# GpSimd adds the squares of two channel tiles in each norm, and the matmul of ones sums the pairs

## What is computed

```python
def rmsnorm(x, gain):
    y = xf * lax.rsqrt(jnp.mean(xf * xf, axis=-1, keepdims=True) + RMS_EPS)
    return (y * gain.astype(jnp.float32)).astype(x.dtype)
...
h = h + 0.5 * swiglu_ffn(rmsnorm(h, ffn1_norm[i]), ffn1_w_in[i], ffn1_w_out[i])
u = rmsnorm(h, mix_norm[i])
y = stick_breaking_attention(u, sb_w_qkv[j], sb_w_o[j], valid)
h = h + y
h = h + 0.5 * swiglu_ffn(rmsnorm(h, ffn2_norm[i]), ffn2_w_in[i], ffn2_w_out[i])
...
h = rmsnorm(h, final_norm)
```

## Time and profile before

| | before |
|---|---|
| median of the runs | 2130.8 us |
| the profiled execution | 2127.97 us, span 2126.2 us |
| PE busy | 1965.9 us, 92% |
| DVE busy | 1097.4 us, 52% |
| POOL busy | 1004.0 us, 47% |
| ACT busy | 686.4 us, 32% |
| mean granted TensorE clock | 0.972 |

### The profile page before, as it was taken

How to read it: one execution, slowest core, us unless ns; L and a number is a source line. 1 busy time by engine, 2 the same in 40 slices (tenths; PEclk the granted TensorE clock), 3 DMA queues, 4 the chain that set the end, 5 groups by cost and what they waited for, 6 DMA issues and landing times.

```text
span 2126.2 us, 35378 instructions
## 1 busy us (share of the span) xinstructions
PE 1965.9 (92%) x12808; PEld 1786.1 (84%) x12808; DVE 1097.4 (52%) x1584; ACT 686.4 (32%) x1226; POOL 1004.0 (47%) x671
## 2 busy tenths in 40 slices
PE   4699999999999985999979999959999999899997
PEld 4699999999999975999978887747777777788886
DVE  5455455554555555334368880174444444454445
ACT  5322222222111124222279882142222222221212
POOL 4554454454534416445467763164454544543340
PEclk8899999999999997999999999979999999999999
DMA  3122222223322200332322212002222222233221
GB/s 120 31 65 84 89 65 84 82 72 125 120 80 83 96 20 21 109 109 95 105 81 67 82 52 60 20 5 84 74 79 84 70 83 84 84 134 109 79 89 79
DMA packets 164783, 167.64 MB, mean 79 GB/s; under 512 B 7920, under 2 KB 130800, under 8 KB 164736
## 3 DMA queue, kind: packets, MB, share of 16 engines
q1 hardware_dynamic: 164736, 166.99, 24.6%
HBM read 126.74 MB, written 40.22 MB: 79 GB/s over the span
## 4 chain that ended last, share of the span: by engine, by line
PE 44%; issue 28%; POOL 19%; ACT 5%; DVE 2%; DMA 1%; POOLq 0%; ACTq 0%; SPq 0%; DVEq 0%
PE psum L1173 14%; PE psum L1174 14%; PE psum L1175 14%; POOL arena L514 13%; POOL arena L522 4%; PE psum L1200 2%; ACT scratch L825 1%; ACT arena L790 1%; DVE scratch L1100 1%; ACT psum L827 1%; DVE psum L896 0%; DMA scratch<-w_out_dram 0%; ACT scratch L875 0%; PE psum L1187 0%; PE psum L1323 0%
## 5 line engine op out<-in xcount | busy, mean ns | idle before, releaser
L1173 PE MATMUL psum<-arena 128*128 128x260 f32 (+4 forms) x4008 | 1280.0, 319 | 126.1 <-POOL arena L522 92.3
L1175 PE MATMUL psum<-arena 128*128 128x260 f32 (+4 forms) x4008 | 1262.8, 315 | 0.0
L1174 PE MATMUL psum<-arena 128*128 128x260 f32 (+4 forms) x4008 | 1261.2, 315 | 0.0
L1173 PEld LDWEIGHTS psum<-arena 128*128 128x128 f32 x4008 | 759.5, 189 | 194.2 <-issue 99.3
L1175 PEld LDWEIGHTS psum<-arena 128*128 128x128 f32 x4008 | 758.8, 189 | 47.4
L1174 PEld LDWEIGHTS psum<-arena 128*128 128x128 f32 x4008 | 758.9, 189 | 45.8 <-issue 3.1
L514 POOL TENSOR_TENSOR arena<-scratch,arena 128x512 fp32r<-128x512 f32 x371 | 512.7, 1404 | 563.4 <-ACT arena L655 563.4
L655 ACT ACTIVATE arena<-scratch 128x512 fp32r<-128x512 f32 x392 | 224.1, 622 | 509.3 <-DMA scratch<-w_in_dram 261.5
L956 DVE SCALAR_TENSOR_TENSOR h<-psum,h 128x260 f32<-128x260 f32 (+1 forms) x528 | 272.1, 516 | 224.2 <-PE psum L1175 224.1
L968 DVE TENSOR_TENSOR scratch<-scratch,psum 128x520 f32<-128x520 f32 (+1 forms) x280 | 193.0, 689 | 375.2 <-PE psum L1175 360.9
L971 DVE TENSOR_TENSOR scratch<-scratch 128x512 f32<-128x512 f32 x212 | 252.1, 1189 | 215.7 <-POOL arena L514 193.2
(11 more groups left out here) (72 smaller groups left out, 1002.1 us busy)
## 6 DMA issues: line engine op xcount, KB each, us to landing
scratch<-w_in_dram SPq DMA_DIRECT2D x88, 512.0 KB, 4.8
scratch<-w_out_dram SPq DMA_DIRECT2D x22, 1024.0 KB, 4.9
qkv<-scratch SPq DMA_DIRECT2D x48, 260.0 KB, 2.1
scratch<-w_qkv_dram SPq DMA_DIRECT2D x24, 512.0 KB, 4.5
scratch<-qkv SPq DMA_DIRECT2D x24, 512.0 KB, 3.8
hidden<-scratch SPq DMA_DIRECT2D x44, 260.0 KB, 2.1
scratch<-hidden SPq DMA_DIRECT2D x11, 1040.0 KB, 5.0
hidden<-scratch SPq DMA_DIRECT2D x44, 256.0 KB, 2.1
```

What stands on the lines that cost most here:

```text
L1173: nc.tensor.matmul(dst, wh, xh, start=start, stop=False, skip_group_check=True)
L1174: nc.tensor.matmul(dst, wh, xl, start=False, stop=False, skip_group_check=True)
L1175: return nc.tensor.matmul(dst, wl, xh, start=False, stop=stop, skip_group_check=True)
```

## The change

Tiles 2p and 2p + 1 form a pair. ACT squares each as before. GpSimd then adds the second to the first, in place in the first's slot, and counts `paired`. PE multiplies only the sum by ones: four instead of eight tiles for each half, the first with `start`, the last with `stop`. The three slots stay. `square` of tile m takes the slot of tile m - 3: if m is even that was the second of a pair and free once GpSimd has added it (`paired`), if m is odd it was the first and free once PE has summed it (`summed`). On GpSimd the adds stand in its program as `pairs`: all eight of FFN1 ahead of `first_weights(FFN1)`, all eight of QKV behind `first_weights(QKV)`, five of FFN2 ahead of `first_weights(FFN2)` and three behind. ACT's own part of `first_weights(FFN2)` stands before the square of tile 11, as before.

```diff
+            def pairs(n, ps):
+                s = norms[n]
+                for p in ps:
+                    first, second = (sq_half[n][:, (2 * p + i) % 3] for i in range(2))
+                    pool.wait_ge(s["squared"], 2 * p + 2)
+                    nc.gpsimd.tensor_tensor(first, first, second, ALU.add).then_inc(s["paired"], 1)
...
+            pairs(FFN1, range(KT))
             first_weights(FFN1)
             units(FFN1)
             down(FFN1)
             first_weights(QKV)
+            pairs(QKV, range(KT))
             units(QKV)
...
+            pairs(FFN2, range(HK + 1))
             first_weights(FFN2)
+            pairs(FFN2, range(HK + 1, KT))
             units(FFN2)
...
                 def square(c, kt, m):
-                    wait(act, s["summed"], m - 2)
+                    if m >= 3:
+                        act.wait_ge(s["summed" if m % 2 else "paired"], (m - 3) // 2 + 1)
...
                 def root(c):
-                    act.wait_ge(s["summed"], KT * (c + 1))
+                    act.wait_ge(s["summed"], HK * (c + 1))
...
                 for at in ats:
+                    if at % 2 == 0:
+                        continue
                     m = c * KT + at
-                    pe.wait_ge(s["squared"], m + 1)
...
+                    pe.wait_ge(s["paired"], m // 2 + 1)
                     for j in range(parts_of):
                         last = nc.tensor.matmul(psum[:, bank + j, 0:cols], ones[:],
-                                                sq_half[n][:, m % 3, j * cols:(j + 1) * cols],
-                                                start=at == 0, stop=at == KT - 1)
+                                                sq_half[n][:, (m - 1) % 3, j * cols:(j + 1) * cols],
+                                                start=at == 1, stop=at == KT - 1)
```

More of the change, by code:

```diff
@@ L274, in build @@
         norms = [{name: sem(f"norm{n}_{name}") for name in
-                  ("squared", "summed", "root", "rstd", "un", "hi", "lo", "lo_pool")} for n in range(3)]
+                  ("squared", "paired", "summed", "root", "rstd", "un", "hi", "lo", "lo_pool")} for n in range(3)]
         ffns = [{name: sem(f"ffn{n}_{name}") for name in
@@ L1193, in sums @@
                 s, bank = norms[n], NORM_BANKS[n][c]
+                half, parts_of = HALF[n], UNIT_CHUNKS[n]
+                cols = half // parts_of
                 for at in ats:
+                    if at % 2 == 0:
+                        continue
                     m = c * KT + at
-                    pe.wait_ge(s["squared"], m + 1)
-                    half, parts_of = HALF[n], UNIT_CHUNKS[n]
-                    cols = half // parts_of
+                    pe.wait_ge(s["paired"], m // 2 + 1)
                     for j in range(parts_of):
                         last = nc.tensor.matmul(psum[:, bank + j, 0:cols], ones[:],
-                                                sq_half[n][:, m % 3, j * cols:(j + 1) * cols],
-                                                start=at == 0, stop=at == KT - 1)
+                                                sq_half[n][:, (m - 1) % 3, j * cols:(j + 1) * cols],
+                                                start=at == 1, stop=at == KT - 1)
                     last.then_inc(s["summed"], 1)
```

## The result

The changed kernel takes 2151.4 us (median of four runs, 2149.9 to 2154.9) against 2130.6 before, ratio 1.010 with a 95% interval of 1.0088 to 1.0112: 20.8 us slower, as against a forecast of 19.6 slower. Its profiled execution took 2150.25 us, 22.3 more than the one before.

What follows compares the result with a forecast made beforehand. Mostly PE's product matmuls and GpSimd's low parts bound the kernel; the sums held 2%, some 43 us. Engines 12.4 + 7.4 - 8.2 = +11.6, plus FFN1's clock 8, gave +19.6: 2150.4 us, range 2139 to 2160.

Steps and rivals of the forecast that it cites:

- The round of three slots: FFN1 and QKV: sum, square, add run serially per pair, 3.30 us a round (4.18 at half clock), against 1.76 before.
- FFN1: FFN1 norm: serial rounds and GpSimd's delayed queue cost 12.4 us on the engines, and PE's lower clock 8 more.
- the clock's part: FFN1: PE at half clock slows sums and transposes, adding 8 us, with bounds 0 and 9.4.
- QKV: QKV norm: each half takes three rounds against seven tiles, 3.7 us longer, 7.4 in all, with the clock at full.
- the second rival: FFN1 and QKV: PE's clock falls in both norms, QKV adding 6.5 us (3 to 10), 2156.9 us; chance 0.28.
- The row at 2108.90: Profiled stretch: after PE had nothing for 2.6 us, the clock had fallen to 1.2 GHz; pattern for the second rival.
- the one at 512.60: Profiled stretch: PE had nothing for 2.8 us, clock stayed at 2.4 GHz; pattern for a held clock, 2142.4 us, chance 0.28.
- FFN2: FFN2 norm: fewer sums between full output groups give back 8.2 us, after waits and the end are taken off.
- the first sum: FFN2: without tile 0's sum, PE goes straight from group 2 to group 3, 4.64 us less.
- the last pair: FFN2's end: the pair's add and waits come between the last square and PE's last sum, 1.5 us more.
- The wait for pair 0 behind split_wo: FFN2: GpSimd adds pair 0 after its last split_wo, at worst 0.1 to 0.3 us of wait, taken as 0.1.
- The faster rival: FFN1 and QKV: the ring doesn't serialize, 14 us gained plus FFN2's 8.2, 2108.6 us; chance 0.04.

Runs made afterwards that it cites:

- e5_fill_gaps: The changed kernel plus eight small unused matmuls behind each pair's sum but a half's last, in FFN1 and QKV: 2144.3 us, ratio 1.0057 to the kernel before.
- e6_qkv_on_dve: Against e3_qkv_only: pairs in QKV alone, three slots, but added by DVE instead of GpSimd; 2137.9 us, ratio 1.0031 to the kernel before.
- e1_ffn2_only: Against the kernel before: tiles paired in the FFN2 norm alone, FFN1 and QKV unchanged; 2120.9 us, ratio 0.994.
- e8_four_slots: Against the change: all three norms in pairs with four slots instead of three; 2126.1 us, ratio 0.9971 to the kernel before.
- e2_ffn1_only: Against the kernel before: tiles paired in the FFN1 norm alone; 2150.3 us, ratio 1.0086.
- e3_qkv_only: Against the kernel before: tiles paired in the QKV norm alone, added by GpSimd; 2139.7 us, ratio 1.0041.
- the last four experiments: The second four of the eight experiment kernels, each timed against the kernel before, whose median beside them was 2131.3 us.

## Why the prediction was right, point by point

**The round of three slots** (forecast 3.30 us at full clock, 4.18 at half) was 3.18 to 3.28 and 4.18 to 4.25. The add took 1.28 us, 0.04 below the row it was taken from. That rounds are serial because of the slots, and not because GpSimd is slow, is what four and eight slots show: the same adds with more slots make the kernel faster than before. A faster add alone (DVE) recovered 3.2 us of QKV's 11.3.

**FFN1** (12.4 for the engines and 8 for the clock, 20.4) measured 17.4. The step mis-sized is the clock's part: 5.0 instead of 8, if the engines' 12.4 holds. e5_fill_gaps bears that out: its 14.0 less some 2 for the two slow rounds is 12. I had both halves at half clock throughout. In fact each half's first round was at full clock, and the transposes between the halves, 32 records in 4.41 us, lost 0.9 us and not up to 3.3, as the clock came back during them. That GpSimd's three combinations of weights queue behind the adds was right: they began at 48.48, as the last add ended.

**QKV** (7.4) measured 11.3. Here the forecast took the clock as full, and this step was wrong: it fell within the third round of each half. What I had priced as a rival at +6.5 happened, at +3.9. With the clock held there, in e5_fill_gaps, the norm cost the 7.4. So the total, 19.6 against 20.8, is nearer than the working deserves, and that is luck: the 3.0 too much in FFN1 and the 3.9 too little in QKV nearly cancel. What happened is the second rival (the clock falls in both norms), at a smaller price. The row at 2108.90 was the better pattern for it than the one at 512.60. The Trainium skill ("TensorE: Matmul & The Clock Gate", section HAM oscillation — how this bites in real kernels) tells of a kernel whose clock dropped in each wait for a transfer between short bursts of matmuls. The trace agrees in kind: the clock was at 0.50 from 18.0 to 29.0 and from 790 to 799. But the waits of that kernel were some 3 to 5 us long, and here waits of 2.1 us (of 1.5 in e6_qkv_on_dve) were enough.

**FFN2** (-8.2) measured -8.5: 4.70 for the first sum (forecast 4.64), 5.36 for six sums (5.2), and 1.53 lost at the last pair (1.5). The wait for pair 0 behind split_wo, 0.1 us in the forecast, did not show.

**The faster rival** needed a round under 2.33 us, and none was. It came true only where the ring was changed. That GpSimd adds at about half DVE's rate (the Trainium skill, "GPSIMD Engine Reference", section Elementwise — side-by-side cycle accounting) agrees with 1.28 against 0.70 us for 520 columns; my estimate from it, 0.66 us a round, came out as 0.62.

**Left over.** The three stretches give 20.1 us, and the two profiled executions differ by 22.3. Up to FFN2's first product matmul (1396.04 before, 1414.68 after) the difference is 18.6; the other 3.6 come in the units and the down-projection of FFN2, whose code is the same. For 2.3 of these the traces show a place. In FFN2's down-projection DVE's adds to h (line 956, after it 970) follow each other every 1.407 us after the change and every 1.393 before, over more than 140 adds in a row, with PE busy throughout at full clock. The longer step is in all three traces of kernels that pair FFN2 in three slots (the change, e1_ffn2_only, e5_fill_gaps), and in none of the other seven. What causes it is open; as each kernel has one trace, it could be the execution and not the kernel. The other 1.3 can be scatter: from the second reciprocal to the down-projection the other eight traces take between 0.2 us less and 1.8 more than the trace before.

## What to carry to other kernels

Before work is handed to an idle engine inside a ring of buffers, count the slots: if an item now holds two slots and passes through one engine more, a ring of three can turn a pipeline into a chain in which every step is paid in full, as it did in FFN1 and QKV, and PE's saved work counts for nothing. One slot more made the difference between loss and gain here. Take the saving only where PE is full, as between FFN2's output groups, leave the last item before a wait of others unpaired, and price the clock too when the change puts waits between short bursts of matmuls.

## What the runs showed of the hardware

The granted clock fell with PE gaps as short as 1.52 us around sums of 1.14 us (e6_qkv_on_dve), and it was at 0.50 in e8_four_slots over 10 us in which PE was busy for 8.6.

The same wait may or may not cost the clock. Behind FFN2's stall of 3.56 us the clock stayed up in the trace before. In all three other traces that leave FFN2 as it was, it fell: the untouched FFN2 stretch took 102.88 us in e2_ffn1_only, 102.75 in e3_qkv_only and 102.93 in e6_qkv_on_dve, instead of 101.16. In e3_qkv_only the stall and what follows it read:

```profile
1303.90:1307.40 3.50, 0.09 (x1) 0.09 (x1) 0.67 (x1) 3.12 (x4) 2.92 (x2) 1.00 0.92 262
1307.80:1311.20 3.40, 3.40 (x8) 2.11 (x7) 0.00 (x0) 0.49 (x1) 2.58 (x3) 0.54 0.00 0
```

So the same code lost 1.6 to 1.8 us or did not. If most executions of the kernel before lose them too, pairing gains some 10 us in FFN2 and not 8.5; its other executions were not traced, so that is not shown.

Runs of one kernel scatter by several us: 2149.9 to 2154.9 after (four runs), 2120.8 to 2129.5 with four slots (ten), and 2128.6 to 2134.4 for the kernel before (the 17 beside the last four experiments). The mean granted clock goes with it in part: of the ten runs with four slots the fastest shows 0.970 and the slowest 0.964, but one of 2123.9 us shows 0.964 as well. Whether the clock causes the scatter was not tested.
